# First feed-forward stage of a decoder trunk: activation table loaded early, turns of x moved between the first products, three chunks turned by TensorE

## What is computed

```python
def _swiglu_ffn(h, w_in, w_out):
    gu = h @ w_in                       # 1024 -> 2 x 2816
    gate, up = jnp.split(gu, 2, axis=-1)
    return (jax.nn.silu(gate) * up) @ w_out
...
x = x + 0.5 * _swiglu_ffn(_rmsnorm(x, ffn_norm[i, 0]), ffn_w_in[i, 0], ffn_w_out[i, 0])
x = x + mixer(_rmsnorm(x, mix_norm[i]))
x = x + 0.5 * _swiglu_ffn(_rmsnorm(x, ffn_norm[i, 1]), ffn_w_in[i, 1], ffn_w_out[i, 1])
```

## Time and profile before

| | us |
|---|---|
| median of 3 runs | 996.33 (994.18 to 997.03) |
| profiled execution | 995.55 |
| its span, first to last instruction | 993.7 |
| TensorE busy in the span | 968.9 (97%) |
| mean granted TensorE clock | 0.991 |

### The profile page before, as it was taken

One profiled execution on the slowest core, in us unless ns is written; L12 is line 12 of the kernel. 1 busy time (PEld: TensorE's weight loads), 2 busy tenths in 40 slices (PEclk: granted clock), 3 DMA queues, 4 the chain that ended last, 5 costly groups with the idle time before them and its releaser, 6 DMA issues.

```text
span 993.7 us, 12480 instructions
## 1 busy us (share of the span) xinstructions
PE 968.9 (97%) x4515; PEld 799.1 (80%) x4515; DVE 778.9 (78%) x1476; ACT 482.0 (49%) x743; POOL 43.8 (4%) x65
## 2 busy tenths in 40 slices
PE   7899999999989999999999999999999899999998
PEld 5788888888977888888888888888876678888887
DVE  4988787877959887878788878787767589787873
ACT  5554444465135453535544535346776565353531
POOL 0200000010200200000000000000203000000000
PEclk9999999999989999999999999999999999999999
DMA  7784545463736545455445454454642134545431
GB/s 242 274 359 176 218 162 230 175 242 120 255 102 254 195 173 210 182 198 196 186 190 211 177 204 191 190 200 147 229 164 107 43 130 192 230 166 215 178 118 43
DMA packets 29661, 185.63 MB, mean 187 GB/s; under 512 B 3504, under 2 KB 3632, under 8 KB 9392
## 3 DMA queue, kind: packets, MB, share of 16 engines
q1 hardware_dynamic: 25056, 169.88, 44.8%
q0 software_dynamic: 4416, 15.09, 4.6%
q10 hardware_dynamic: 144, 0.07, 0.1%
HBM read 183.98 MB, written 1.05 MB: 186 GB/s over the span
## 4 chain that ended last, share of the span: by engine, by line
PE 87%; DVE 7%; ACT 3%; issue 1%; POOL 1%; DMA 1%; DVEq 0%; ACTq 0%
PE pg L419 16%; PE pg L423 16%; PE pg L425 16%; PE acc L419 11%; PE acc L425 11%; PE acc L423 11%; PE acc L612 3%; DVE w_lo L1175 3%; PE pt L508 1%; POOL mix L377 1%; ACT w_hi L817 1%; DVE mix L1477 1%; DMA diags<-in_conv_diags 1%; DVE mix L1291 0%; ACT mix L989 0%
## 5 line engine op out<-in xcount | busy, mean ns | idle before, releaser
L1175 DVE TENSOR_TENSOR w_lo<-raw,w_hi 128x1024 fp32r<-128x1024 f32 x316 | 369.3, 1221 | 21.8 <-ACT w_hi L817 20.5
L817 ACT CAST w_hi<-raw 128x1024 fp32r<-128x1024 f32 x316 | 312.1, 1049 | 13.7 <-DMA raw<-in_units 13.6
L419 PE MATMUL pg<-w_hi,a_hi 128*128 128x512 f32 x720 | 281.4, 391 | 0.0
L425 PE MATMUL pg<-w_hi,a_lo 128*128 128x512 f32 x720 | 280.2, 389 | 0.0
L423 PE MATMUL pg<-w_lo,a_hi 128*128 128x512 f32 x720 | 280.1, 389 | 0.0
L1291 DVE STREAM_TRANSPOSE mix<-hs 32x128 f32<-32x128 f32 x640 | 193.5, 302 | 9.6
L419 PEld LDWEIGHTS pg<-w_hi,a_hi 128*128 128x128 f32 x720 | 135.3, 188 | 28.1 <-issue 0.4
L425 PEld LDWEIGHTS pg<-w_hi,a_lo 128*128 128x128 f32 x720 | 135.2, 188 | 28.2
L423 PEld LDWEIGHTS pg<-w_lo,a_hi 128*128 128x128 f32 x720 | 135.2, 188 | 27.6
L1283 DVE SCALAR_TENSOR_TENSOR hs<-pg,rstd,hs 128x256 f32<-128x256 f32 x80 | 38.4, 484 | 100.0 <-ACT hs L862 100.0
L862 ACT ACTIVATE hs<-pg,rstd 128x256 f32<-128x256 f32 x80 | 37.9, 475 | 159.3 <-PE pg L425 159.3
(11 more groups left out here) (140 smaller groups left out, 638.4 us busy)
## 6 DMA issues: line engine op xcount, KB each, us to landing
raw<-in_units SPq DMA_DIRECT2D x158, 1024.0 KB, 5.3
diags<-in_conv_diags POOLq DMA_DIRECT2D x20, 512.0 KB, 4.7
raw<-in_units SPq DMA_DIRECT2D x8, 256.0 KB, 5.4
gain<-in_ffn_norm POOLq DMA_DIRECT2D x3, 512.0 KB, 4.5
xs<-in_x SPq DMA_DIRECT2D x4, 256.0 KB, 4.9
gain<-in_mix_norm POOLq DMA_DIRECT2D x2, 512.0 KB, 5.3
xg<-in_conv_b_in POOLq DMA_DIRECT2D x2, 512.0 KB, 4.3
out_y<-xs SPq DMA_DIRECT2D x4, 256.0 KB, 2.0
```

The costliest lines, as they stand in the source:

```text
L419: mm = pe.matmul(dst[j], stat_hi, m_hi, start=first, stop=False)
L425: mm = pe.matmul(dst[j], stat_lo, m_hi, start=False, stop=last)
L817: nc.scalar.copy(w_hi[n % RING][:, cols], raw[n % RAW][:, cols]).then_inc(hi_done, 1)
L1175: nc.vector.tensor_tensor(w_lo[n % RING][:, cols], raw[n % RAW][:, cols], w_hi[n % RING][:, cols].bitcast(F32), ALU.subtract).then_inc(lo_ ...
```

## The change

It touches stage 0 alone, in five ways:

1. ScalarE runs a Silu of one column of the constant tile before it waits for anything of the input, so the activation table with Silu is loaded first.
2. `WARM` goes from (7, 4) to (5, 2).
3. The turns of the second, third and fourth block of x stand one product piece earlier each: before pieces 1, 3 and 5 of unit 0 in place of 2, 4 and after the last.
4. ScalarE and DVE take the quarters of unit 1 in between the tiles of blocks 2 and 3. On ScalarE the squares of half 0 come ahead of unit 3's casts and those of half 1 behind them; on DVE `token_factors` comes behind unit 3's rests.
5. Chunks 0, 1 and 2 of stage 0 are turned by TensorE (`by_tensor`), as the last chunk of each stage was: chunk 0 before piece 3 of unit 3, chunks 1 and 2 before piece 2 of their own `second_unit` call, that is in units 4 and 7.

```diff
-WARM = (7, 4)
+WARM = (5, 2)
+FIRST_CHUNKS = 3
...
+        def by_tensor(s, c):
+            return c == FCH - 1 or s == 0 and c < FIRST_CHUNKS
...   (TensorE, enter)
-                    first_unit(0, 0, banks, {2: lambda: turn(0, 0, 1), 4: lambda: turn(0, 1, 0)}, norm=0)
-                    turn(0, 1, 1)
+                    first_unit(0, 0, banks, {1: lambda: turn(0, 0, 1), 3: lambda: turn(0, 1, 0), 5: lambda: turn(0, 1, 1)}, norm=0)
...   (TensorE, ffn)
-                def turn_last():
-                    c = FCH - 1
+                def turn_gated(c):
                     pe.wait_ge(chunk_out, 2 * (o0 + c + 1))
...
-                    first_unit(n + 1, 1, banks, {}, i)
+                    first_unit(n + 1, 1, banks, {3: lambda: turn_gated(0)} if first and by_tensor(s, 0) else {}, i)
                     hidden_ready(c - 1, i)
-                    second_unit(s, n + 2, left((c - 1) % 2), first, False, {2: turn_last} if last else {}, i)
+                    second_unit(s, n + 2, left((c - 1) % 2), first, False, {2: lambda: turn_gated(c)} if by_tensor(s, c) else {}, i)
...   (ScalarE, hidden; DVE's hidden has the same choice of source)
-                                   pt[:, 0, :] if last else hT.rearrange("p k n -> p (k n)")).then_inc(h_hi_done, 1)
+                                   pt[:, 0, :] if by_tensor(s, c) else hT.rearrange("p k n -> p (k n)")).then_inc(h_hi_done, 1)
...   (ScalarE, stage 0)
+                    act.wait_ge(warm_set, 1)
+                    nc.scalar.activation(warm, h_hi[:, 0, 0, 0:1].bitcast(F32), ACT.Silu)
                     act.wait_ge(first_loaded, 16)
...   (ScalarE; DVE has the same with a_lo and w_lo)
-                    for t in range(TT):
-                        for k in range(4):
-                            tile(1, t, k)
                     for k in range(4):
-                        quarter(1, k)
+                        tile(1, 0, k)
+                    quarter(1, 0)
+                    quarter(1, 1)
+                    for k in range(4):
+                        tile(1, 1, k)
+                    quarter(1, 2)
+                    quarter(1, 3)
...   (DVE)
-                    token_factors(s)
                     rest_half(3, 0)
                     rest_half(3, 1)
+                    token_factors(s)
...
-                    if not last:
+                    if not by_tensor(s, c):
                         turn_hidden(c, i)
```

## The result

| | before | after |
|---|---|---|
| median, us | 995.99 (994.18 to 997.03, 4 runs) | 986.6 (984.98 to 987.52, 4 runs) |
| profiled execution, us | 995.55 | 984.98 |
| its span, us | 993.7 | 983.2 |
| first product of unit 5 ("the mark") | 48.03 | 38.20 |

The ratio is 0.9904, interval 0.989 to 0.9918: 9.4 us or 0.94% faster, clear of the 0.3% that count as no change. The forecast was 988.1 (985.4 to 990.9).

What follows compares the result with a forecast made beforehand. TensorE, busy in 97% of the span, was taken as the bound, with its idle time, low clock and start to win. Gone 11.25 less added 3.05 gave net 8.2 us, hence 988.1 us, range 985.4 to 990.9.

Steps and rivals of the forecast that it cites:

- The start: First ScalarE tile at 5.75, first product 7.5, third piece 9.95: minus 2.15 us, of which 1.3 is the table load.
- The idle time of 2.85 and of 2.8, and the low clock behind each: TensorE's waits before unit 1 (2.85) and unit 4 (2.8) go, with 1.7 and 1.75 us of low clock behind them.
- The turns: Turns of chunks 0, 1 and 2 moved onto TensorE: each adds 0.45 us.
- The stall in unit 4: TensorE's turn of chunk 1 waits for its gating: plus 0.4 us, bounds 0 and 1.9.
- The loads: Loads of units 3, 4 and 5 are issued 2 to 5 us sooner, each there before its cast is due.
- The clock at the start: With less warm-up the first products may meet the low clock: plus 1.3 us, between 0 and 2.6.
- Chunk 2: Its turn adds 0.45 us; its gating is covered while units 9 and 10 are cast in time.
- Clock up and no stall: Rival: clock up from the first product and no stall, gain 9.9 us, hence 986.4 us; chance 0.22.
- The turn that waits: Rival: a late load of unit 7 makes the turn in unit 4 wait nearly 5 us more, 990.5 likely; chance 0.13.
- The slower case: Rival: clock never comes up in units 0 and 1; low through unit 3 it is 9.7 us slower, 1006; chance 0.02.
- Gain given back later: Rival: at four later stage changes one more clock fall gives 990 us, one fewer 986.4; chance 0.15.
- the table's 1.3: Loading ScalarE's activation table ahead, while it has nothing to do, starts its first tile 1.3 us sooner.

Runs made afterwards that it cites:

- e9: The kernel before, with only chunk 0 turned by TensorE; median 992.23 us.
- e1: The kernel after, without the early Silu of one column, so the table is loaded late; median 988.37 us.
- e3: The kernel after, with chunks 0 to 2 turned by DVE again; median 991.75 us.
- e11: The kernel after run once more, unchanged; median 985.02 us, ratio to before 0.9877.
- e2: The kernel after, with the turns of x back before pieces 2 and 4 of unit 0 and behind its last; median 991.78 us.
- e8: The kernel after, with the orders of ScalarE and DVE as before; median 987.68 us.
- e10: The kernel before, with only the early Silu of one column added; median 994.18 us.

## Why the prediction was right, point by point

**The start.** ScalarE's first tile at 5.74 (5.75 forecast), first product 7.48 (7.5), third piece 9.94 (9.95). The minus 2.15 holds.

**The idle time of 2.85 and of 2.8, and the low clock behind each.** Gone, all four. Here the prediction had a mechanism, a wait and a clock behind it, and the rows show both. Gating of chunk 0 ended at 26.55 (26.3), TensorE's turn stood at 28.01 (27.9), `h_lo` was done at 30.59 (31.0) and wanted at 31.90 (31.7). e9 shows the second pair alone: 4.12 against 2.8 + 1.75 - 0.45 = 4.1.

**The turns.** 28.01 to 28.36, and the next product 0.1 slower: 0.45 each, as taken.

**The stall in unit 4.** Gating of chunk 1 ended at 34.90 (34.8 forecast); TensorE idled 0.18 by the row, 0.34 behind the pace of its starts, for 0.4 taken.

**The loads.** Units 3, 4 and 5 were to be there before their casts; that of unit 5 held ScalarE for 0.17 at 25.21. Unit 2, left out of the account, held it for 0.43 at 16.05, so Silu of chunk 0 stood at 24.20 and not at 23.6. It cost TensorE nothing at chunk 0, whose gating was 1.5 ahead of its turn.

**The clock at the start** was the one term without a row. I took 1.3 between 0 and 2.6. It is not one number: in the profile of after it was 0, and the mark there is 38.20 against the 38.08 that the sum gives without it (48.03 - 11.25 + 0.9 + 0.4); in the second profile of the same kernel it was 1.4 at the mark, 1.75 from the first product on. The median of 986.6 lies 1.5 below the forecast. Of that, the term's size is one part, and the scatter behind the mark, larger than the term, is the other; I can't divide them. The prediction also quotes the Trainium skill ("TensorE: Matmul & The Clock Gate", "Part 4: PE-mode transpose") for turns that do not count as work for the clock, and finds one stretch of rows in line with it. Another profile speaks against it: in e1, after 4.77 idle and 16 turns with no product among them, the granted clock was 0.50 up to 288.5 and 1.00 from 289.0, and the first product there runs at full pace already:

```profile
285.44 1.95 PE L664 MATMUL pg<-first,xg 128*128 128x128 f32 x8 [4.77 <-DVE xg L1419]
287.18 1.89 PE L664 MATMUL pt<-first,xg 128*128 128x128 f32 x8
289.04 0.72 PE L425 MATMUL acc<-w_hi,a_hi 128*128 128x512 f32 x2
```

e3 shows the same at 292.44. Where page and trace differ the trace decides; no number of the forecast rested on it.

**Chunk 2.** No wait at its turn (51.81, without a bracket), as forecast.

**The rivals.** "Clock up and no stall" (986.4) describes the clock of the profiled execution and its small stall, the forecast describes e11 (its mark would be 39.4, and was 39.62). The turn that waits: 0.17 to 0.57 in all runs with three chunks and the new turns of x, 1.18 in e2, never the 5 of a load in the burst. The slower case needed 48 products in the low clock; the longest stretch at the start was 12 (e2). Gain given back later: from mark to end nothing was lost.

**What was right by luck.** The terms up to the mark came out as taken, save that of the clock at the start. That the total lies in the range is less certain than it looks: by its mark e11 is the execution that the forecast describes, yet its median of 985.02 lies 0.4 outside the range of 985.4 to 990.9. With the four executions of the result it lies inside. The range allowed 1 for the scatter of a median, and two medians of the same kernel differ by 1.6.

The prediction also gave the 2.85 of idle ahead of unit 1 to the start as a whole and no price to the edits in it, save the table's 1.3. The runs do, and they do not add up one by one. With the orders alone (e2, old turns) TensorE enters unit 1 without a wait; with the new turns alone (e8, old orders) it waits 0.49. So either edit takes most of the 2.57 away, and no run has one of them alone on the kernel before. What the turns bring beyond that is an earlier start of everything behind them: 3.3 at the fourth block's turn, and most of it reaches the mark by way of ScalarE and the turn of chunk 1. An engineer who had asked which single edit matters most would have had no answer from the sum. By the runs it is the turn of chunk 0 by TensorE (4.1 on the kernel before), then the order of the turns of x (about 3 on the kernel after), then the orders and the table with about 1 each.

## What to carry to other kernels

Where several engines feed the first products, look for the queue that runs without a stop from some event to the first dependent result (here ScalarE, from the fourth block's tiles to Silu); the event that starts it is worth moving ahead, here nearly one for one, as long as the bound engine waits for the end of that queue. A transpose moved from a busy engine onto the bound one pays only where its consumer waits: once here, for chunk 0, and not for chunks 1 and 2. And where the bound engine's clock can fall, an idle time removed is worth more than its length: 2.8 of waiting came with 1.75 of slow products, 3.8 with 2.9. Last, take the price of a part from a fixed event in the trace, and look at the same kernel twice before believing a median.

## What the hardware showed

- **The clock at the start differs per execution.** Same kernel, first pieces at 2.4 GHz in one profile and at 1.2 GHz in the next, 1.4 us apart at the mark.
- **It can also fall after it was up, and later than the idle time.** e1: up at 8.42 behind a wait of 2.46, down at about 9.2, up again by 12.5. Before: idle from 17.4 to 19.96, down only at about 21.3. Up to the mark, the low clock came behind each of the seven waits of 2.46 to 3.71 (two each in before and e10, one each in e1, e3 and e9). That is a count of rows; no run varied the length of a wait alone.
- **It came up behind turns alone.** e1 and e3: 16 turns after 4.8 idle, then the first product at full pace; in before only the pair at 297.89 is, the seventh product.
- **A table load cost 1.28 us and the next activation followed within 0.02**, at 1.18, 5.38, 25.73 and in both loads of before (5.75 and 28.81).
- **The landing of the first small load varied** by 0.9 us between executions (TensorE's first turn of x started between 4.16 and 5.06), which moves the whole start and the mark with it.
